# An expert's down-projection bias moved to the middle of its products, with undivided down chunks and roots that take scale and bias

## What is computed

```python
x = x + gt_m * mix_lat                       # Fourier heads and RG-LRU heads, each with an RMSNorm
h = modulate(rmsnorm(x, g_norm_ffn[i]), sh_f, sc_f)
gu = xb @ w_gu[e] + b_gu[e]                  # an expert's rows: 1024 -> 2048
gt = jnp.minimum(gu[:, :D_FF], SWIGLU_LIMIT)
up = jnp.clip(gu[:, D_FF:], -SWIGLU_LIMIT, SWIGLU_LIMIT)
act = (up + 1) * (gt * jax.nn.sigmoid(SWIGLU_ALPHA * gt))
out = act @ w_down[e] + b_down[e]            # 1024 -> 1024
y = y + gt_f * (out * gate), at the rows' tokens
return rmsnorm(x, g_final)                   # x * rsqrt(mean(x * x) + 1e-6) * g
```

## Time and profile before

| | |
|---|---|
| Median of 3 runs | 1431.67 us (1430.12 to 1432.78) |
| Profiled execution | 1433.7 us, of which its span 1431.9 us |
| Granted PE clock over the span | 0.957 |
| Busy | PE 1312.6 us (92%), DVE 959.8 us (67%), ACT 592.3 us (41%), POOL 218.0 us (15%) |
| Loaded or stored by DMA | 473.28 MB, mean 331 GB/s |
| Items | 45; the first output at 318.8 us of the span, the last at 1408.5 us |

### The profile page before, as it was taken

One profiled execution on the slowest core, in us unless ns is written; L12 is line 12 of the kernel. 1 busy time (PEld: TensorE's weight loads), 2 busy tenths in 40 slices (PEclk: granted clock), 3 DMA queues, 4 the chain that ended last, 5 costly groups with the idle time before them and its releaser, 6 DMA issues.

```text
span 1431.9 us, 25034 instructions
## 1 busy us (share of the span) xinstructions
PE 1312.6 (92%) x6267; PEld 541.6 (38%) x6267; DVE 959.8 (67%) x1588; ACT 592.3 (41%) x636; POOL 218.0 (15%) x149
## 2 busy tenths in 40 slices
PE   4699869699999999999989998899999999999993
PEld 2487438533333333333323332233333333333331
DVE  2999899756666666666546664566666666666664
ACT  3333752434444444444234343334343434343433
POOL 1741144011111111110110100010101010101010
PEclk9799969889999999999999999899999999999997
DMA  9664231789999999599999999998997199999993
GB/s 381 219 233 176 103 140 59 302 304 385 404 398 403 360 411 394 186 376 403 401 405 396 410 397 404 408 408 342 390 400 290 39 386 401 405 397 348 409 409 142
DMA packets 87780, 473.28 MB, mean 331 GB/s; under 512 B 14289, under 2 KB 14801, under 8 KB 37585
## 3 DMA queue, kind: packets, MB, share of 16 engines
q1 hardware_dynamic: 76930, 454.16, 79.6%
q0 software_dynamic: 10832, 18.90, 5.8%
HBM read 462.00 MB, written 18.35 MB: 335 GB/s over the span
## 4 chain that ended last, share of the span: by engine, by line
PE 69%; DVE 11%; DMA 6%; SPq 6%; issue 4%; ACT 2%; POOL 1%; DVEq 0%; ACTq 0%; POOLq 0%
PE ps L1498 40%; PE ps L1510 15%; SPq L317 5%; PE ps L1520 2%; DVE osb L1219 2%; DMA wm<-in_w_mod 2%; DMA ring<-in_w_down 2%; DMA ring<-in_w_gate_up 2%; PE ps L1480 2%; PE ps L1291 2%; PE ps L1292 2%; PE ps L1293 2%; PE ps L1490 1%; DVE ab L1178 1%; DVE ub L1175 1%
## 5 line engine op out<-in xcount | busy, mean ns | idle before, releaser
L1498 PE MATMUL ps<-window,xT 128*64 128x512 f32 x2880 | 649.1, 604 | 0.0
L1004 DVE COPY window<-ring 128x2048 f32 x360 | 441.5, 1226 | 261.0 <-PE ps L1498 140.1
L1498 PEld LDWEIGHTS ps<-window,xT 128*64 128x64 f32 x2880 | 201.3, 139 | 388.2 <-issue 387.9
L740 ACT ACTIVATE window<-ring 128x2048 f32 x180 | 338.9, 1906 | 4.7 <-DMA ring<-in_w_down 3.4
L1510 PE MATMUL ps<-window,aT 128*64 128x512 f32 x1440 | 329.3, 599 | 0.0
L734 ACT ACTIVATE sg<-gb 128x256 f32<-128x256 f32 x90 | 37.5, 417 | 647.1 <-DVE gb L1171 523.3
L548 POOL DMA_INDIRECT out_parts<-osb,idx_c x46 | 79.8, 1734 | 796.9 <-DVE osb L1219 782.2
L1510 PEld LDWEIGHTS ps<-window,aT 128*64 128x64 f32 x1440 | 100.0, 138 | 185.1 <-issue 180.8
L1171 DVE TENSOR_SCALAR gb<-ps 128x256 f32<-128x256 f32 x90 | 38.1, 424 | 124.2 <-PE ps L1498 124.2
L533 POOL DMA_INDIRECT xg<-h_rows,idx_n x46 | 45.0, 979 | 253.6 <-DVE idx_n L1051 203.1
L1490 PE MATMUL ps<-bias_w,pick 128*128 128x512 f32 x135 | 56.1, 471 | 20.0 <-DVE osb L1219 16.1
(11 more groups left out here) (298 smaller groups left out, 1123.3 us busy)
## 6 DMA issues: line engine op xcount, KB each, us to landing
ring<-in_w_gate_up SPq DMA_DIRECT2D x256, 1024.0 KB
ring<-in_w_down SPq DMA_DIRECT2D x128, 1024.0 KB
wm<-in_w_mod SPq DMA_DIRECT2D x4, 2048.0 KB, 21.5
wm_a<-in_w_mod SPq DMA_DIRECT2D x4, 2048.0 KB, 9.0
wm_b<-in_w_mod SPq DMA_DIRECT2D x4, 2048.0 KB, 8.8
win<-in_w_in SPq DMA_DIRECT2D x3, 2048.0 KB, 20.1
x_in<-in_x SPq DMA_DIRECT2D x1, 2048.0 KB, 10.4
wo_f<-in_w_out SPq DMA_DIRECT2D x1, 2048.0 KB, 7.4
```

What stands on the lines that cost most here:

```text
L740: A(window[c % NW][:, :, :, :], ring_chunk(c, p), ACT.Copy).then_inc(S["moved_b"], 1)
L1004: V.tensor_copy(window[c % NW][:, :, :, :], ring_chunk(c, p)).then_inc(S["moved_a"], 1)
L1498: last = MMUL(ps[M * j:M * (j + 1), h, :].rearrange("m (g n) -> m g n", g=2), xT[:, k, :], window[c % NW][:, k % CK, :, j * GW:(j + 1) * G ...
```

## The change

The product that opens bank 2 with the down bias, and its wait for the output of the item before, move from the head of an item to its middle, ahead of the first transposes. The first half of the down products is no longer split around the second transposes: all of it is ahead of them. DVE waits for its own output copy ahead of `hold_numbers`, which overwrites the gate that the copy reads. In all four norms ACT's root takes the scale 1/n and the bias epsilon (a new column of the constants), reads the sum of squares itself, and DVE's instruction for the mean is gone with its semaphore; the last stage's loop on DVE is `scaled(t)` alone. The same edit takes the mean out of `rstd_heads` and `ffn_norm` on DVE.

```diff
--- before.py
+++ after.py
...
@@ -574,9 +575,10 @@
                     if t:
                         act.wait_ge(S["ssq_in"], t)
                     A(junk[:, :], src[:, t - t0, :], ACT.Square, accum_out=ss[:, t:t + 1]).then_inc(S["ssq_in"], 1)
-                act.wait_ge(S["mean_in"], 1 + (t0 > 0))
-                A(ss[:, t0:t1], ss[:, t0:t1], ACT.Sqrt).then_inc(S["root_in"], 1)
-
+                act.wait_ge(S["ssq_in"], t1)
+                A(ss[:, t0:t1], ss[:, t0:t1], ACT.Sqrt, bias=const("eps"), scale=1.0 / D).then_inc(S["root_in"], 1)
+
+            act.wait_ge(S["ld_cst"], 16)
...
             def root_heads(i):
-                act.wait_ge(S["mean_heads"], i + 1)
-                A(rsf[:, 2 + i, :], rsf[:, i, :], ACT.Sqrt).then_inc(S["root_heads"], 1)
+                act.wait_ge(S[("ssf_done", "ssr_done")[i]], 1)
+                A(rsf[:, 2 + i, :], ps[:, 0, TL * i:TL * (i + 1)], ACT.Sqrt, bias=const("eps"), scale=1.0 / DF).then_inc(S["root_heads"], 1)
...
             def root_x2(t):
-                act.wait_ge(S["mean_ffn"], t + 1)
-                A(rsf[:, 3, t:t + 1], rsf[:, 2, t:t + 1], ACT.Sqrt).then_inc(S["rt_ffn"], 1)
+                act.wait_ge(S["ssq_ffn"], t + 1)
+                A(rsf[:, 3, t:t + 1], ss[:, t:t + 1], ACT.Sqrt, bias=const("eps"), scale=1.0 / D).then_inc(S["rt_ffn"], 1)
...
             def root_out(t):
-                act.wait_ge(S["mean_out"], t + 1)
-                A(rsf[:, 1, t:t + 1], rsf[:, 0, t:t + 1], ACT.Sqrt).then_inc(S["rt_out"], 1)
+                act.wait_ge(S["ssq_out"], t + 1)
+                A(rsf[:, 1, t:t + 1], ss[:, t:t + 1], ACT.Sqrt, bias=const("eps"), scale=1.0 / D).then_inc(S["rt_out"], 1)
...
             def norm(t0, t1, i, src, dst):
-                dve.wait_ge(S["ssq_in"], t1)
-                V.tensor_scalar(ss[:, t0:t1], ss[:, t0:t1], 1.0 / D, EPS, ALU.mult, ALU.add).then_inc(S["mean_in"], 1)
                 dve.wait_ge(S["root_in"], i + 1)
...
@@ -1200,6 +1195,7 @@
                     second(4)
                     second(5)
                     dve.wait_ge(S["gathered"], 16 * b + 16)
+                    dve.wait_ge(S["o_copied"], b + 1)
                     hold_numbers(b + 1)
...
             dve.wait_ge(S["ld_gnf"], 32)
-            def mean(t):
-                dve.wait_ge(S["ssq_out"], t + 1)
-                V.tensor_scalar(rsf[:, 0, t:t + 1], ss[:, t:t + 1], 1.0 / D, EPS, ALU.mult, ALU.add).then_inc(S["mean_out"], 1)
-
             def scaled(t):
...
             for t in range(TL):
-                mean(t)
-                if t:
-                    scaled(t - 1)
-            scaled(TL - 1)
+                scaled(t)
...
@@ -1529,18 +1518,17 @@
                     pe.wait_ge(S["pick_ready"], b + 1)
                     bias(0)
                     bias(1)
-                    pe.wait_ge(S["o_copied"], b + 1)
-                    bias(2).then_inc(S["bias_used"], 1)
                     pe.wait_ge(S["xT_ready"], b + 1)
                     gate_up(0, 0, 8, b)
                     gate_up(1, 0, 4, b)
+                    pe.wait_ge(S["o_copied"], b + 1)
+                    bias(2).then_inc(S["bias_used"], 1)
                     act_to_channels(0, b)
                     gate_up(1, 4, 8, b)
                     pe.wait_ge(S["aT_ready"], 2 * b + 1)
-                    down(0, 0, 2, b)
+                    down(0, 0, 4, b)
                     act_to_channels(1, b)
                     rows_to_channels(16 * b + 32)
-                    down(0, 2, 4, b)
                     pe.wait_ge(S["aT_ready"], 2 * b + 2)
                     down(1, 0, 4, b)
```

More of the change, by code:

```diff
@@ L60 @@
 for _name, _n in (("ident", P), ("cd", P), ("neg_sd", P), ("ones", P), ("slot", P), ("before", P),
-                  ("expert", NE), ("place", NE), ("expert_of_row", CG), ("part", 1), ("index", 1), ("token", 2 * TL)):
+                  ("expert", NE), ("place", NE), ("expert_of_row", CG), ("part", 1), ("index", 1), ("eps", 1), ("token", 2 * TL)):
     CST[_name] = (_at, _at + _n)
@@ L94, in constants @@
     put("index", p[:, None])
+    put("eps", EPS)
     put("place", np.array([*PLACE_OF_RANK, 0])[None])
@@ L296, in build @@
             ld_zm0 ld_zm1 ld_bc ld_gnf ld_wo0 ld_wo1 ld_wr ld_bias dve_step act_step
-            bias_hi csil_ready mod_done mod_copied mod_turned zeroed t_done t_by_act t_by_dve mean_in
-            root_in mean_ffn film_ready bf_ready ssq_in xs_ready hl_by_act hl_by_dve
+            bias_hi csil_ready mod_done mod_copied mod_turned zeroed t_done t_by_act t_by_dve
+            root_in film_ready bf_ready ssq_in xs_ready hl_by_act hl_by_dve
             hc_hi hc_t hc_lo hl_t win_hi_ready win_lo_ready mm_done mm_copied xr_done xr_copied conv_done
@@ L301, in build @@
             dft_done cf_copied ssf_done sp_ready ix_ready a_ready th_ready q_ready w_ready root_ready
-            rg_ready sqr_ready ssr_done mean_heads root_heads rsf_ready cf_lo catR_hi_ready catR_lo_ready
+            rg_ready sqr_ready ssr_done root_heads rsf_ready cf_lo catR_hi_ready catR_lo_ready
             wo_hi_ready wo_lo_ready pf_done pf_copied pr_done pr_read x2_ready ssq_ffn rt_ffn lg_copied
@@ L307, in build @@
             bias_used held g_ready act_ready sel_ready idx_ready cur_ready pick_ready s_sig aT_ready
-            xT_ready o_copied gathered scattered mean_out ssq_out
+            xT_ready o_copied gathered scattered ssq_out
             rt_out out_ready stored"""
@@ L962, in _, with rstd_heads @@
                 V.tensor_tensor(Um[:, 0, t, NC:], Um[:, 0, t, NC:], gelu[:, t, :], ALU.mult).then_inc(S["rg_ready"], 1)
-            def rstd_heads(i, name):
-                dve.wait_ge(S[name], 1)
-                V.tensor_scalar(rsf[:, i, :], ps[:, 0, TL * i:TL * (i + 1)], 1.0 / DF, EPS, ALU.mult, ALU.add).then_inc(S["mean_heads"], 1)
+            def rstd_heads(i):
                 dve.wait_ge(S["root_heads"], i + 1)
@@ L971, in _ @@
             round_wo(1)
-            rstd_heads(0, "ssf_done")
+            rstd_heads(0)
             for t in range(RT):
@@ L994, in ffn_norm @@
             def ffn_norm(t):
-                dve.wait_ge(S["ssq_ffn"], t + 1)
-                V.tensor_scalar(rsf[:, 2, t:t + 1], ss[:, t:t + 1], 1.0 / D, EPS, ALU.mult, ALU.add).then_inc(S["mean_ffn"], 1)
                 dve.wait_ge(S["rt_ffn"], t + 1)
@@ L1006, in _ @@
             gated_fourier(0)
-            rstd_heads(1, "ssr_done")
+            rstd_heads(1)
             dve.wait_ge(S["rsf_ready"], 2)
```

## The result

The changed kernel takes 1416.01 us (1415.33 to 1419.75, 4 runs) against 1432.03 us for the kernel before in the same comparison: ratio 0.9888, 95% interval 0.9873 to 0.9903, so 16.0 us faster. The forecast was 1422.3 with a range down to 1416.5: right in sign, too small by more than a third of the gain. A second comparison gave 0.9898 (0.9883 to 0.9913) and 1417.55 us against 1432.32, so 14.8 us.

What follows compares the result with a forecast made beforehand. PE's list was taken to bound 32 items and full DMA engines the stretch between. 32 x 0.24 = 7.7 us plus 1.7 us in the last stage made 9.4 us, so 1431.7 - 9.4 = 1422.3 us, range 1416.5 to 1429.

Steps and rivals of the forecast that it cites:

- Which regime binds, and how many items count: In the loop: PE's list paces 32 items, which gain; between them full DMA engines bind and nothing is gained.
- The boundary: Between items: gate products follow the second bias directly, without the third; 0.49 to 0.59 us saved per item, 0.55 taken.
- The middle bias: Down bias ahead of the first transposes: costs PE 0.31 us per item, ends 0.23 and 0.43.
- The second transposes' wait: PE's wait for the activations before the second transposes: undivided down chunks remove it, 0.12 us gained per item.
- Chunk 11, the first failing step: Down's last chunk, copied by ACT: 1.3 us slack becomes a 0.06 wait plus restart of some 0.05; 0.12 lost per item.
- T: Start of an item's second transposes; chunk 11's copy was to end at T + 2.74, PE to want it at T + 2.73.
- 0.24 + 0.12 - 0.12 = 0.24 us: Gain per item: both bias places net, plus the second transposes' wait, minus chunk 11; pace from 23.91 to 23.67 us.
- The starved stretch: Loop items from resumed loading to the output at 930.32: DMA engines bind, PE's saving is waited for weights, nothing gained.
- the cheap ones: Rivals: chunk 11 never late, 0.36 us per item, 1418.5; with cheapest bias 0.48, 1414.7. Chance below 1419: 0.13.
- The late chunk 11 (0.44): Rival: chunk 11 follows as in an item with late weights, -0.08 us per item, 1432.6; chance within 0.2%: 0.10.
- starved groups elsewhere: Rival: full loading before 590 and behind 930 binds too, half the items give nothing, 1426.2; 0.11 with dear bias.
- the slow copy of `aT`: Rival: the copy starts 0.90 us behind the second transposes' start, PE waits 0.86 for chunk 11, 1446; slower: 0.06.

Runs made afterwards that it cites:

- The run with chunk 11 later: The changed kernel with one more 128x128 ScalarE copy between the copy of `aT` and chunk 11: median 1420.22 us (2 runs).
- the doubled bias: The changed kernel with the down bias added twice in the middle of the item: ratio 0.9935 to the kernel before.
- The kernel in which GpSimd waits: The changed kernel with GpSimd's four subtractions for win_lo started only after `film_ready`: median 1419.49 us.

## Why the prediction was off

**Which regime binds, and how many items count:** right. The changed kernel is paced by PE in 32 items, starved in the two same groups.

**The boundary:** 0.59 measured, 0.55 taken. **The middle bias:** 0.28 measured, 0.31 taken. With both, 0.31 (the run with the bias alone) where 0.24 stood. **The second transposes' wait:** 0.12, right; it is gone from the chain.

**Chunk 11, the first failing step:** the mechanism right, its size wrong. 0.12 was taken, 0.055 measured. The copy ends at T + 2.74 as computed. The fault is on PE's side: the first pair behind the row transposes takes 0.05 longer than the others (a row of two lasts 0.65, not 0.60), so PE asks at T + 2.78, not T + 2.73, and the wait is 0.01 with a restart of 0.05. The run with chunk 11 later shows that the place is the right one, to a hundredth.

The sum that failed is therefore "0.24 + 0.12 - 0.12 = 0.24 us", which measured 0.365. Three of its entries erred to the same side: the boundary saved 0.04 more, the middle bias cost 0.03 less, and chunk 11 cost 0.065 less, the largest. Over 32 items that is 11.8 instead of 7.7 us, 4.1 of the missing 6.6.

**The starved stretch:** the second failing step, "what PE saves is waited for weights", so nothing gained. It gained 1.8. A chunk has landed when the last of its 16 semaphore increments arrives; the traces have these times. For the last chunk of each starved group and the output that ends the group:

| Profile | second group: landing, behind the 13th output | output behind the landing | first group: output behind the landing |
|---|---|---|---|
| before (down divided) | 318.16 | 6.32, clock low | 6.20, clock low |
| roots alone (down divided) | 317.52 | 6.49, clock low | 6.39, clock low |
| bias alone (down divided) | 317.27 | 6.28, clock low | 4.65, clock high |
| the changed kernel | 318.40 | 4.32, clock high | 4.32, clock high |
| all nine with three or four k of down ahead of the transposes | 316.51 to 318.49 | 4.31 to 4.32, clock high | 4.31 to 4.32, clock high |

The landing is pinned, as the forecast said: 0.24 later in the changed kernel, and no order among the twelve. What it had wrong is that the output follows from the landing alone. It comes 2.0 us sooner behind it. In the changed kernel the chain has only chunk copies and down's last four pairs (the load in its first line is chunk 10's, landed at 914.78):

```profile
885.95 28.83 DMA ring<-in_w_down
...
915.14 1.92 ACT window L742
917.06 0.26 ACT aT L732
...
917.63 1.92 ACT window L742
...
919.59 1.94 PE ps L1499 x8
```

Chunk 11 lands at 917.27, is copied from 917.63, and its four pairs end at the output, 921.58. In the kernel before, the chain of the same item ends on PE, with all twelve pairs that stand behind the second transposes:

```profile
922.23 0.44 PE ps L1520 x2
922.67 0.64 PE ps L1480 x8
923.31 6.98 PE ps L1510 x24
```

ACT had chunk 11's copy done at 926.27, so PE set this output and not the landing. PE was late for two reasons. One is the clock; the windows are of the kernel before, at those products, and of the changed one:

```profile
923.20:926.60 3.40, 3.40 (x10) 0.99 (x10) 1.09 (x2) 3.08 (x4) 0.00 (x0) 0.50 1.02 419
```

```profile
908.00:922.00 14.00, 11.29 (x58) 3.61 (x56) 8.87 (x13) 7.16 (x8) 0.00 (x0) 1.00 1.01 411
```

PE had 1.2 GHz for 3.4 us behind the last landing before, and 2.4 GHz throughout after. The other is the order: with down divided, four pairs more stand behind the transposes, which wait for the activations. The first group's last item separates the two. Before, and in the run with the bias alone, whose down is divided as before but whose clock stayed high there:

```profile
759.51 1.04 PE ps L1480 x8
760.55 6.44 PE ps L1510 x24
```

```profile
755.16 0.64 PE ps L1481 x8
755.80 5.30 PE ps L1511 x24
```

The same instructions take 7.48 and 5.94 us, 1.5 us for the clock alone. In the one group end that divided down had at the high level the output is 4.65 behind the landing, undivided 4.32: 0.33 for the order. So of the 2.0 us in the second group some 1.7 are the clock's.

In all, the kernel before spent 34 us of the starved stretch at the low level, the changed one none, its repetition 3.4; but ahead of the last landing it cost nothing that shows: the landing is at 318.16 with it and at 318.40 without. Behind it the three kernels with divided down had the low level in five of their six group ends, and the nine others in none of eighteen. (The run with down alone had it at the head of the second group's last item, 898.08 to 904.91, and its output still came 4.32 behind the landing.) That these orders keep the high level there is a pattern of twelve profiles; why is not shown.

The two failing steps make 5.9 of the missing 6.6 us. The rest, 0.7, is less than the 1.2 us by which the two comparisons differ.

**The last stage:** 1.7 forecast, 1.66 to 1.67 measured in every profile with the roots. The other three roots gave nothing that repeats.

**The front part:** forecast at nothing; 2.5 us in this profile. It goes with the clock. PE's windows around the small transposes of the modulation, before and after:

```profile
38.00:40.20 2.20, 1.55 (x17) 1.53 (x17) 0.60 (x1) 0.94 (x1) 0.00 (x0) 0.76 1.04 371
```

```profile
38.00:40.20 2.20, 1.20 (x17) 1.12 (x17) 0.93 (x4) 0.94 (x1) 0.00 (x0) 0.95 1.04 374
```

Where the low level set in at 40.0 to 40.7 (the changed kernel twice, the doubled bias, the later chunk 11) the first output came at 316.3 to 317.0. Where it set in at 37.8 to 39.3, and came once more near 69 us (seven profiles, four of them with the new roots), it came at 318.1 to 319.3. (The kernel in which GpSimd waits is left out of this count.) Identical front parts are on both sides, so the 2.5 us are not the change's to keep.

The traces show a way for the first 1.0 us of it. In the four early profiles the transposes take 1.15, and the first of DVE's two scalings behind them runs in 0.17, ahead of GpSimd's first subtraction; the second overlaps it and takes over 2 us. In the seven late ones the transposes take 1.54 to 1.87, and both scalings overlap the subtraction, at 1.9 to 2.4 us each:

```profile
40.13 0.17 DVE L820 SCALAR_TENSOR_TENSOR sc<-sc,pc 128x8 f32<-128x8 f32 x1
```

```profile
40.50 2.28 DVE L820 SCALAR_TENSOR_TENSOR sc<-sc,pc 128x8 f32<-128x8 f32 x1
```

The first line is of the changed kernel, the second of the one before; each is the first of its two scalings. In the late profiles ACT waits for the second scaling and GpSimd's next step for ACT, 1.6 us behind the subtractions, so that this step starts at 51.5 to 52.0; in the early ones it follows them after 0.2, at 50.5 to 50.9. All eleven fit; no run forces it, since the kernel meant to do so also moved GpSimd.

Without the first line of the table the profiles give 15.2; the medians gave 16.0 and 14.8. Whether the roots make the early state more likely stays open; no kernel without them showed it, in three profiles.

**What of the rivals:** the measured 1416.0 lies in the span of the cheap ones (1418.5 to 1414.7), but that is luck in part. Chunk 11 never late, their premise, is not what came: it costs 0.055. The boundary and the middle bias came out 0.07 better than taken and make up for it, so that the item's 0.365 meets their 0.36. Of the 2.8 us over their gain of 13.2 the starved stretch gave 1.8, which they put at nothing. The late chunk 11 (0.44), starved groups elsewhere, and the slow copy of `aT` did not come: the items behind the 25th output stay at 23.55, and the copy starts 0.48 behind the transposes once ACT is idle.

## What to carry to other kernels

A small product that waits for another engine should stand where that engine has long been done and next to products of its own array shape; here the same move was worth 0.31 us per item beside the transposes, and gave back 0.30 of it among the 64-column products. After such a move, count the new slack on every queue that was shifted, with the longer first instruction behind a change of shape: 0.05 us decided whether chunk 11 was late. And where a group of items ends on a late load, count what stands behind the landing, order and clock included: a pinned landing does not pin the output. The kernel with the transposes after three k (1415.39 us; items 23.50) is the version to keep, by a margin that only the item pace shows.

## What the runs showed of the hardware

Being starved can cost twice. The clock was granted at 1.2 GHz in stretches of 3.4 and 6.8 us in and behind the waits for weights, and an item's head that ran into one took 12.20 us (from 902.63) for 48 products that otherwise take 10.45 (from 931.63). Only where such a stretch lay behind a group's last landing did the time grow by it, by 1.5 to 1.8 us. A product of 512 columns behind another of its shape costs 0.225 us and 0.28 as the first behind 64-column pairs; leaving and re-entering the 64-column shape costs 0.30 in all. DVE's scaling of 128x8, 0.17 us by itself, took 1.9 to 2.4 us while GpSimd's subtraction ran. And the same program's front part ends some 2 us earlier or later, together with where the clock's low stretches fall, so a single profile can't credit a change with that.
